# Weighing the first two slot groups of a PEER stage ahead of the second tile's query turns and the third query's product

## What is computed

```
def peer(h, w_q, sub_keys, u, v):
    q = (hf @ w_q).reshape(T, PEER_HEADS, 2, PEER_KEY_DIM // 2)
    sc = jnp.einsum('thpc,pkc->thpk', q, sub_keys)
    v1, i1 = lax.top_k(sc, PEER_TOPK)
    cand = v1[:, :, 0, :, None] + v1[:, :, 1, None, :]      # 16 x 16 candidates
    top, pos = lax.top_k(cand, PEER_TOPK)                   # 16 experts for a token and head
    gates = jax.nn.softmax(top, axis=-1)
    a = jax.nn.gelu(jnp.einsum('cd,ced->ce', xc, u[ec]))    # a dot with each expert's row of u
    return jnp.einsum('ce,ced->cd', gc * a, v[ec])          # the weighted sum of its rows of v
```

## Time and profile before

| | before |
|---|---|
| median of 3 runs | 914.76 us (912.7 to 915.89) |
| the profiled execution's own time | 921.77 us |
| its span, first to last instruction | 920.0 us |
| mean granted TensorE clock | 0.962 |
| TensorE (PE) busy | 839.7 us (91%) |
| VectorE (DVE) busy | 643.3 us (70%) |
| ScalarE (ACT) busy | 413.4 us (45%) |
| GpSimd (POOL) busy | 392.1 us (43%) |
| all DMA | 300.66 MB, mean 327 GB/s |

### The profile page before, as it was taken

One profiled execution on the slowest core, in us unless ns is written; L12 is line 12 of the kernel. 1 busy time (PEld: TensorE's weight loads), 2 busy tenths in 40 slices (PEclk: granted clock), 3 DMA queues, 4 the chain that ended last, 5 costly groups with the idle time before them and its releaser, 6 DMA issues.

```text
span 920.0 us, 15506 instructions
## 1 busy us (share of the span) xinstructions
PE 839.7 (91%) x5704; PEld 538.5 (59%) x5704; DVE 643.3 (70%) x1467; ACT 413.4 (45%) x1060; POOL 392.1 (43%) x307
## 2 busy tenths in 40 slices
PE   9998999999999868797999999979887898999985
PEld 8998998789987723354665565545343433333321
DVE  5433687375566898888989999988988644444465
ACT  6434656345555556455554455533333322222253
POOL 1000045314001467475554555566656754455460
PEclk9999999999999998898999999998987999999988
DMA  8887624246452989999999999999999999999993
GB/s 305 221 219 184 220 102 146 84 184 241 171 205 98 361 311 418 418 382 417 414 408 397 415 415 415 414 416 397 419 414 400 404 416 417 416 416 417 418 417 142
DMA packets 56179, 300.66 MB, mean 327 GB/s; under 512 B 12466, under 2 KB 15910, under 8 KB 23746
## 3 DMA queue, kind: packets, MB, share of 16 engines
q0 software_dynamic: 37152, 218.57, 58.6%
q1 hardware_dynamic: 16120, 78.23, 23.3%
q10 hardware_dynamic: 2832, 2.88, 2.1%
HBM read 348.00 MB, written 1.54 MB: 380 GB/s over the span
## 4 chain that ended last, share of the span: by engine, by line
PE 44%; DMA 26%; DVE 15%; ACT 8%; issue 6%; POOL 1%; another core or an unknown queue 0%; POOLq 0%; SPq 0%; DVEq 0%; ACTq 0%
PE y L1206 12%; DMA late_ring<-in_experts,arena 10%; DMA arena<-in_experts,arena 9%; DMA raw<-in_panels 6%; DVE late_ring L2249 6%; PE ps L1256 5%; PE ps L820 4%; PE ps L821 4%; PE ps L822 4%; DVE w_lo L1801 3%; PE y L1289 3%; PE ps L863 2%; ACT w_hi L1383 2%; ACT diag L1617 2%; PE ps L1277 2%
## 5 line engine op out<-in xcount | busy, mean ns | idle before, releaser
L2459 POOL DMA_INDIRECT arena<-in_experts,arena x148 | 199.2, 1346 | 150.6 <-PE ps L1209 112.7
L2249 DVE CUSTOM_DVE_ANT_0 late_ring<-arena 128x1024 f32<-128x1024 f32 x160 | 194.4, 1221 | 74.2 <-DMA arena<-in_experts,arena 68.1
L1206 PE MATMUL y<-arena,diag 64*64 64x512 f32 x584 | 149.3, 632 | 29.8 <-ACT diag L1617 29.2
L1209 PE MATMUL ps<-arena,diag 64*64 64x512 f32 x632 | 165.5, 647 | 0.0
L1603 ACT ACTIVATE acts<-dots 128x2 f32<-128x2 f32 x125 | 25.2, 202 | 254.9 <-DVE dots L2249 249.3
L1801 DVE TENSOR_TENSOR w_lo<-raw,w_hi 128x2048 fp32r<-128x2048 f32 x36 | 84.9, 2360 | 77.3 <-ACT w_hi L1383 77.3
L2249 DVE CUSTOM_DVE_ANT_0 late_ring<-late_ring,arena 128x1024 f32<-128x1024 f32 x80 | 97.2, 1220 | 29.5 <-DMA late_ring<-in_experts,arena 27.3
L2459 POOL DMA_INDIRECT late_ring<-in_experts,arena x63 | 83.6, 1326 | 62.0 <-PE ps L1209 49.2
L1383 ACT CAST w_hi<-raw 128x2048 fp32r<-128x2048 f32 x37 | 70.5, 1905 | 65.8 <-DMA raw<-in_panels 52.5
L1206 PEld LDWEIGHTS y<-arena,diag 64*64 64x64 f32 x584 | 36.1, 137 | 109.1 <-issue 57.9
L1206 PE MATMUL y<-late_ring,diag 64*64 64x512 f32 x304 | 79.8, 648 | 20.9 <-ACT diag L1617 20.8
(11 more groups left out here) (356 smaller groups left out, 1817.7 us busy)
## 6 DMA issues: line engine op xcount, KB each, us to landing
raw<-in_panels SPq DMA_DIRECT2D x40, 1024.0 KB, 4.9
arena<-in_panels SPq DMA_DIRECT2D x6, 1024.0 KB, 7.0
x<-in_up SPq DMA_DIRECT2D x12, 512.0 KB
late_ring<-in_up SPq DMA_DIRECT2D x12, 512.0 KB
x<-in_experts SPq DMA_DIRECT2D x12, 512.0 KB
late_ring<-in_experts SPq DMA_DIRECT2D x12, 512.0 KB
arena<-line_scratch ACTq DMA_DIRECT2D x8, 320.0 KB, 8.5
arena<-in_experts,arena POOLq DMA_INDIRECT x148
```

What stands on the lines that cost most here:

```text
L1206: straight = pe.matmul(y[rows, t, cols], diag[rows, a % DIAGS, rows], slot(a)[rows, down], start=False, stop=False, skip_group_check=True)
L1209: across = pe.matmul(ps[to, half, :], diag[rows, b % DIAGS, rows], slot(b)[rows, down], start=first, stop=False, skip_group_check=True)
L2249: i = nc.vector.tensor_tensor_reduce(row if n < len(FIRST_BUFFERS) else products[s % GROUP], row, h_rows[:, u // PEER_HEADS, :], 1.0, 0.0, ...
L2459: nc.gpsimd.indirect_dma_start(out=slot(n), out_offset=None, in_=experts, in_offset=bass.IndirectOffsetOnAxis(ap=expert_rows(u)[:, s:s + 1 ...
```

## The change

It moves work of unit 0 forward, and some work of queries 0 to 2 back. On TensorE `use_pair` of group 0 comes straight after the query products of tile 1; the turns and scores of heads 0 and 1 of tile 1 follow, then group 1, and only then the product of head 2 for tile 0. The later pieces of head 2 move back by two groups (one for the second product). On ScalarE `expert_softmax(0)` comes sooner, `weigh(0, 0)` stands between the two copies of the query products, and the copies for head 2 follow TensorE's new order. On VectorE the dots of slots 0 and 1 and unit 0's gates come before the low part of the panel of head 2. `LATE_PRODUCTS` now begins at the first of tile 1's turns, so that banks 0 and 1 are free when group 0 needs them.

```
-LATE_PRODUCTS = PLACE["qpeer2_0"]
+LATE_PRODUCTS = PLACE["qturn0_1"]
...  (TensorE)
-            for step in (query_product, query_turn, query_scores):
-                for h in range(2):
-                    step(h, 1)
+            for h in range(2):
+                query_product(h, 1)
...
+            for name in LAST_IN_CROSSED:
+                pe.wait_ge(taken[TAKER[name]], taken_count(name))
+            use_pair(0, 0, True)
+            for step in (query_turn, query_scores):
+                for h in range(2):
+                    step(h, 1)
...
-            for i in range(last_unit):
+            for i in range(1, last_unit):
-                if i == 0:
-                    query_product(2, 0)
-                    for name in LAST_IN_CROSSED:
-                        pe.wait_ge(taken[TAKER[name]], taken_count(name))
-                if i == 4:
-                    query_product(2, 1)
+                if i in (2, 5):
+                    query_product(2, i // 5)
...
-                if i in (0, 5):
-                    query_turn(2, i // 5)
-                if i in (1, 6):
-                    query_scores(2, i // 6)
+                if i in (2, 6):
+                    query_turn(2, i // 6)
+                if i in (3, 7):
+                    query_scores(2, i // 7)
...  (ScalarE)
             split_panel(PANELS.index("qpeer2"))
+            expert_softmax(0)
             take_query_tile(1, 0)
...
-            expert_softmax(0)
-            for take_step in (take_query_tile, take_turned_query, take_scores_tile):
+            take_query_tile(0, 1)
+            weigh(0, 0)
+            take_query_tile(1, 1)
+            for take_step in (take_turned_query, take_scores_tile):
...
-                if i == 0:
+                if i == 2:
                     take_query_tile(2, 0)
                     take_turned_query(2, 0)
-                if i == 1:
+                if i == 3:
                     take_scores_tile(2, 0)
-                if i == 4:
+                if i == 5:
                     take_query_tile(2, 1)
-                if i == 5:
+                if i == 6:
                     take_turned_query(2, 1)
                     scale_rows(1)
-                if i == 6:
+                if i == 7:
                     take_scores_tile(2, 1)
...  (VectorE)
-            split_panel(PANELS.index("qpeer2"))
+            dve.wait_ge(h_rows_ready, 1)
+            dot(0)
             turned_rows(1)
             rows_mean(1)
+            dot(1)
+            gate_weights(0)
+            split_panel(PANELS.index("qpeer2"))
             rows_rstd(1)
-            gate_weights(0)
-            dve.wait_ge(h_rows_ready, 1)
```

More of the change, by code:

```diff
@@ L1716, in final_root @@
                                      ACT.Sqrt).then_inc(root_ready, 1)
-            for i in range((UNITS - 1) * TOPK // GROUP):
+            for i in range(1, (UNITS - 1) * TOPK // GROUP):
                 weigh(i // (TOPK // GROUP), i % (TOPK // GROUP))
@@ L2377, in _ @@
                     dve.wait_ge(h_rows_ready, 2)
-                dot(n)
+                if n >= GROUP:
+                    dot(n)
                 if n in GATES_AT:
```

## The result

The change made the kernel slower. Its median is 920.47 us (5 runs, 919.4 to 924.36) against 914.26 us of the kernel before, measured beside it; the ratio is 1.0067 [1.0044, 1.0091]. Timed again in another session it was 921.35 us, ratio 1.0072 [1.0045, 1.0099]. The profiled execution took 919.62 us, with a span of 917.8 us. (Every execution here takes about 1.8 us outside its span, so these are no part of the 7 us by which that one lay above its median.)

A forecast was written before the change was run, and what follows sets the result against it. DMA was taken as the bound behind 404 us, with thin places ahead of it at 322 to 340 and 390 to 404. Group 9's 0.9 plus the clock's 0.8 made +1.7 on 914.76: 916.5 us, range 911.5 to 919.5.

The forecast's parts named there:

- no measurable change: The main case for the whole kernel, as summed: between 913.8 and 917.4 us, chance 0.51.
- Group 0's weights, group 1, slot 10: Start of unit 0: group 0 at 314.7, group 1 at 321.0, slot 10's gather at 317.5, 5.1 us sooner.
- The new wait: VectorE at unit 2's first route step waits 2.7 us, until 333.4, for head 2's scores, which come 4.7 us later.
- Group 9: TensorE starts group 9 at 360.0 instead of 359.06, 0.9 us later, after a series of handoffs from group 6.
- The knot: VectorE's wait for head 3's scores until 379.22, before unit 3's first route step; it moves 0.9 us later.
- the lead: Gathers issued sooner: 5.1 us at slot 10, 4.3 at slot 12, 0.3 at slot 18; about 3 us as a mean.
- its 1.4s are in the old times: On TensorE, the old stretch's slow-clock delays, 1.4 us a time, are already in the old times.
- TensorE has no gap to give: From group 9 to head 3's scores TensorE is busy, so group 9's 0.9 us delay passes on in full.
- The clock: Slow clock behind TensorE's new gaps, 1.4 us a time: taken as 0.8 us, bounds 0 and 4.2.
- The gaps run slow: Slower rival: two slow 1.4 us stretches on TensorE's path make +3.7 us (918.5), three +5.1 (919.9); chance 0.26.
- Slot 0 did not land late: Rejects the slower rival that VectorE's first dot ends behind 307.4; at 2 us late, +3.7 us (918.5), chance 0.06.
- The lead is kept: Faster rival: group 9 comes before 359 and DMA keeps 3 us (911.8) or all 5.9 (908.9); chance 0.17.

The follow-up runs named there:

- first_late: The changed kernel with head 2's pieces for tile 1 one group forward, at the places of before, tile 0's left late; 915.26 us, ratio 1.0000.
- warm_before_2: Repeat of the kernel before with TensorE's gaps ahead of groups 1, 2, 6, 7 and 9 filled by matmuls adding zeros; 914.87 us, ratio 1.0002.

## Why the prediction was wrong

I forecast 916.5 us, between 911.5 and 919.5, with no measurable change as the likeliest; the kernel took 920.5. By its own steps:

- *Group 0's weights, group 1, slot 10.* Right to 0.1 us for slot 10 (317.5 less 4.44 is 313.1, measured 313.03), and 1.1 us too soon for slot 12, since group 1 ran slow.
- *The new wait.* It is there, 4.61 us where I had 2.7; with the gap ahead of group 1 filled it is 2.92 us. The series of products, turns and handoffs was thus summed well, and the rest is group 1's slow stretch. first_late has the same wait and lost nothing against the kernel before.
- *Group 9.* I had 360.0, that is 54.1 us behind the turned rows. Measured with the gaps filled 52.1, with them open 56.4 and 56.7. So my full-clock series was 2.0 us too long, and the slow stretches ahead of group 9 add 4.3 to 4.6. But I set this full-clock series against an old time that had slow stretches in it. With both kernels filled group 9 comes 3.6 to 3.9 us later (52.1 against 48.6 and 48.2), not 0.9, and the step 1.9 to 2.3 us later. Group 9 of warm_before_2 in TensorE's timeline:
```profile
353.21 0.65 PE L1210 MATMUL y<-late_ring,diag 64*64 64x512 f32 x2 [1.40 <-ACT diag L1621]
```
- *The knot.* It moved, the rate at 390 to 404 us fell as said, and the lead was handed back, most of it sooner than I had it: at 20 to 60 us behind the turned rows. But "its 1.4s are in the old times" compared a new series with an execution of before that had drawn three slow groups; another has one, and reaches group 9 4.4 us sooner. And "TensorE has no gap to give" from group 9 on held only for that execution: with a sooner group 9 the step is bound by VectorE's dots and by transfers as well, so that 4.4 us at group 9 became 1.7 at the step.
- *The clock*: the step that failed. "So I take 0.8 us", with an upper bound of 4.2 for three stretches on the path. Four run slow, in both profiles, each costs 1.4 to 2.6 us as the scores and turns behind a group slow down too, and together they are 5.7 to 7.5 us. My argument that part of it falls beside waits for VectorE held for 0.6 us. Against the kernel before, whose own slow stretches delay its step by 2 to 4 us, the clock's share of the later step is thus about 3.5 us where I had 0.8, and the series' about 2 where I had 0.9: 5.6 together, by the means of two profiles each, against 6.2 in the medians. The medians of the filled kernels would put all of it on the clock; between the two the record doesn't decide. Either way the term for the clock is the one that was far too small. The sentence on the Trainium skill (TensorE: Matmul & The Clock Gate, "What's actually happening"), that idling halves the clock, taken strictly, was nearer the truth than my own term; the traces of the changed kernel agree with it for 8 of 10 gaps, not always.
- *The rivals.* "The gaps run slow" was the right mechanism and too small: +5.1 for three stretches against a measured +6.2. Slot 0 did not land late: its dot ended at 301.8, and my limit was 307.4 less 4.4. "The lead is kept" did not come true: DMA was ahead in the first 20 us and had given it back by 60 us.

What the change does, then: the pieces of head 2 used to stand where TensorE would wait for ScalarE. Taken out and put further back, they leave longer gaps (1.9, 1.8, 3.3, 2.8 and 3.5 us, against 1.8, 1.9, 2.8, 1.9 and 1.6), and behind a gap of 2.8 us or more TensorE was slow in 17 of 20 cases.

## What to carry to other kernels

Work that moves out of a gap on TensorE can cost twice, for the gap that it leaves and for the half clock behind it; here each slow stretch took 1.4 to 2.6 us more, mostly 1.6. Price a new gap of about 3 us in a serial stretch that way, price the old order at the same clock as the new one, and try matmuls that add zeros in it before judging the order. Ahead of a sum made against one profiled execution, see whether its time lies near the median of the timed ones, and if it does not, ask which of its slow stretches are chance. And a wait that stands out in the profile after (4.6 us here) is not yet the cause: leave it in place and take away the rest.

## What the hardware showed that I had not expected

A gap does not always bring the slow clock. Over groups 0 to 9 of the eleven profiles in which gaps were open, a group behind a gap of 2.8 us or more ran slow in 17 of 20 cases, behind a gap of 1.8 or 1.9 us in 15 of 24, and the same gap of the same kernel came out either way (group 1 of before, 1.80 us: slow in one profile, at full clock in the other). Between profiles of one order the starts of the groups agree to 0.03 us until the first difference in the clock.

Filling gaps does not always help: in the kernel before, where one to three groups ran slow, it brings the step from 71.6 or 73.3 us to 69.2 or 69.6 and the median nowhere (0.9996 and 1.0002). In the profiles those 2 to 4 us do reach the end: 610.4 and 610.5 us from the turned rows to the end of the span, 612.2 and 614.1 unfilled. Why the medians don't show them stays open.
